# Moving the weight loads of a two-layer decoder step from SyncE's DMA queue to ScalarE's, and four weight tiles later in each chunk

## The reference

```python
# layer 0: differential attention, sample rows read a paged K/V cache of 2048 tokens per sequence
proj = rms_norm(x, norm_pre) @ w_in              # 2048 x 8192: q, k, v, gate
p = softmax(q1 k1^T - slope*dist) - lam * softmax(q2 k2^T - slope*dist)
x = x + rms_norm((head_rms_norm(p @ v) * silu(gate)) @ w_out, norm_post)
# layer 1: retention in chunks of 128, sample rows read and write a recurrent state
proj = rms_norm(x, norm_pre) @ w_in_ret          # 2048 x 12288: q, k, v (512 a head), gate
o = (q k^T * decay) v + q S * decay ;  S = decay*S + k^T v
x = x + rms_norm((head_rms_norm(o) * silu(gate)) @ w_out_ret, norm_post)
```

## Time and profile before

| | us |
| --- | --- |
| median of 3 runs | 4121.02 |
| lowest and highest | 4120.16, 4127.6 |
| the profiled execution's own time | 4107.18 |
| its span | 4105.4 |
| TensorE busy | 3767.5 (92%) |
| ScalarE busy | 1138.2 (28%) |
| VectorE busy | 1427.7 (35%) |

### The profile page before, as it was taken

How to read it: one execution, slowest core, us unless ns; L and a number is a source line. 1 busy time by engine, 2 the same in 40 slices (tenths; PEclk the granted TensorE clock), 3 DMA queues, 4 the chain that set the end, 5 groups by cost and what they waited for, 6 DMA issues and landing times.

```text
span 4105.4 us, 69674 instructions
## 1 busy us (share of the span) xinstructions
PE 3767.5 (92%) x26880; PEld 3289.5 (80%) x26880; DVE 1427.7 (35%) x2278; ACT 1138.2 (28%) x1905; POOL 125.1 (3%) x76
## 2 busy tenths in 40 slices
PE   2998999999999998999579999999999999989996
PEld 2987777777777776776579989898988888879996
DVE  2234333333343334333432423233333334233333
ACT  4233223322332333231332222222222222222221
POOL 0000000200020002002000000000000000000000
PEclk7999999999999998999789999999999999999998
DMA  2355777677767775764323334343424243343323
GB/s 75 106 173 164 233 214 236 190 232 221 238 191 235 218 231 182 228 191 147 113 73 112 125 117 134 111 145 95 154 80 157 79 153 104 133 140 116 106 83 129
DMA packets 466203, 632.41 MB, mean 154 GB/s; under 512 B 39441, under 2 KB 288914, under 8 KB 462738
## 3 DMA queue, kind: packets, MB, share of 16 engines
q1 hardware_dynamic: 401538, 555.71, 43.4%
q10 hardware_dynamic: 64336, 72.24, 5.1%
HBM read 555.61 MB, written 70.65 MB: 153 GB/s over the span
## 4 chain that ended last, share of the span: by engine, by line
PE 53%; DVE 3%; ACT 2%; issue 2%; ACTq 2%; DMA 1%; POOL 1%; SPq 1%; DVEq 0%; POOLq 0%
PE low_banks L832 42%; PE high_banks L832 7%; PE high_banks L835 3%; POOL area L1644 1%; DVE area L1583 1%; ACTq L1245 1%; DVE WL L1328 1%; ACT XH L1055 1%; DVE area L1605 1%; DMA area<-in_cache_v 0%; ACTq L1215 0%; ACT WH L1055 0%; ACTq L1214 0%; PE low_banks L835 0%; ACT area L1055 0%
## 5 line engine op out<-in xcount | busy, mean ns | idle before, releaser
L832 PE MATMUL low_banks<-XH,WH 128*128 128x288 f32 x6656 | 1527.0, 311 | 46.2 <-DVE XL L1333 16.3
L832 PE MATMUL low_banks<-XH,WL 128*128 128x288 f32 x6656 | 1431.9, 297 | 0.0
L832 PE MATMUL low_banks<-XL,WH 128*128 128x288 f32 x6656 | 1428.8, 296 | 0.0
L832 PEld LDWEIGHTS low_banks<-XH,WH 128*128 128x128 f32 x6656 | 1072.5, 191 | 197.0 <-issue 154.5
L832 PEld LDWEIGHTS low_banks<-XH,WL 128*128 128x128 f32 x6656 | 1077.4, 190 | 0.0
L832 PEld LDWEIGHTS low_banks<-XL,WH 128*128 128x128 f32 x6656 | 1077.3, 190 | 0.0
L1328 DVE TENSOR_TENSOR WL<-WR,WH 128x1024 fp32r<-128x1024 f32 x416 | 509.3, 1224 | 965.2 <-ACT WH L1055 964.1
L1055 ACT ACTIVATE WH<-WR 128x1024 fp32r<-128x1024 f32 x416 | 439.9, 1057 | 981.4 <-PE low_banks L832 672.7
L832 PE MATMUL high_banks<-area 128*32 128x512 f32 (+7 forms) x3696 | 670.2, 553 | 45.2 <-issue 17.0
L835 PE MATMUL high_banks<-eye_sb,area 128*128 128x128 f32 (+2 forms) x3048 | 458.8, 287 | 203.2 <-ACT area L1055 150.1
L835 PEld LDWEIGHTS high_banks<-eye_sb,area 128*128 128x128 f32 (+2 forms) x3048 | 362.7, 147 | 346.4 <-issue 182.2
(11 more groups left out here) (93 smaller groups left out, 901.1 us busy)
## 6 DMA issues: line engine op xcount, KB each, us to landing
area<-in_cache_k SPq DMA_DIRECT2D x512, 256.0 KB, 4.1
area<-in_cache_v SPq DMA_DIRECT2D x512, 256.0 KB, 3.9
WR<-in_w_in_ret SPq DMA_DIRECT2D x192, 512.0 KB, 3.6
WR<-in_w_in_attn SPq DMA_DIRECT2D x128, 512.0 KB, 5.2
out<-area ACTq DMA_DIRECT2D x73, 512.0 KB, 3.9
area<-in_state_ret SPq DMA_DIRECT2D x64, 512.0 KB, 5.5
WR<-in_w_out_ret SPq DMA_DIRECT2D x64, 512.0 KB, 3.4
WR<-in_w_out_attn SPq DMA_DIRECT2D x32, 512.0 KB, 4.9
```

Source lines behind the costliest of these rows:

```text
L832: return nc.tensor.matmul(out, a, b, start=start, stop=stop, skip_group_check=True)
```

## The change

`load_w` becomes a stage of ScalarE, and stands behind tile 6 of a chunk in place of tile 2. The split stays where it is. What the load waits for, what it moves and where it goes stay the same; the three loads of `begin` keep their places in the list, now on ScalarE.

```diff
@@ Projections.tile
         out = [Stage("project", **a)]
         if i == 2 and n + 1 < len(self.chunks):
-            out += [Stage("split_w", slot=(n + 1) % 2)] + self.load(n + 3)
+            out += [Stage("split_w", slot=(n + 1) % 2)]
+        if i == 6:
+            out += self.load(n + 3)
@@ block.sync
-            def load_w(g, slot, w, row, col):
-                sp.wait_ge(sem["w_lo"], c.before("w_lo"))
-                sp.dma_start(WR[:, slot, :, :], weights[w][:, row:row + CH, col:col + 256]).then_inc(sem[f"w_in{slot}"], 16)
@@ block.scalar
+            def load_w(g, slot, w, row, col):
+                act.wait_ge(sem["w_lo"], c.before("w_lo"))
+                act.dma_start(WR[:, slot, :, :], weights[w][:, row:row + CH, col:col + 256]).then_inc(sem[f"w_in{slot}"], 16)
```

More of the change, by code:

```diff
@@ L814, in x_tile @@
                     load_x(t, None)
-            run(sp, c, dict(relay_area=all_done(sp, c), relay_loads=all_done(sp, c), load_w=load_w, load_x=load_gated, load_k=load_k, load_v=load_v, load_bias_sample=load_bias_sample,
+            run(sp, c, dict(relay_area=all_done(sp, c), relay_loads=all_done(sp, c), load_x=load_gated, load_k=load_k, load_v=load_v, load_bias_sample=load_bias_sample,
                                   load_bias_prompt=load_bias_prompt, load_head=load_head, load_state=load_state,
@@ L1284, in store_x @@
                 act.dma_start(dst, xt[0:R, t % 2, :]).then_inc(sem[f"x_out{t % 2}"], 16)
-            run(act, c, dict(relay_area=all_done(act, c), split_w=split_w, split_x=split_x, split_s=split_s, evacuate=evacuate, p_exp=p_exp, p_transpose=p_transpose,
+            run(act, c, dict(relay_area=all_done(act, c), load_w=load_w, split_w=split_w, split_x=split_x, split_s=split_s, evacuate=evacuate, p_exp=p_exp, p_transpose=p_transpose,
                                 natural=natural, store_natural=store_natural, store_gated=store_gated, page=page,
```

## The result

The changed kernel takes 4131.4 us (median of 20 runs, 4124.5 to 4135.6) against 4119.6 us for the kernel before on the same chip (20 runs). The ratio is 1.0025, with a 95% interval of 1.0018 to 1.0032. So it is slower: by 11.8 us between the medians, by 10.3 us by the ratio, and between 7.4 and 13.2 by its interval. Predicted were 4114 us, range 4104 to 4127.

The account below looks back on a forecast made before the run. TensorE was taken to set the time, with queue changes moving only its stalls. Terms −2.5 − 2.8 − 4.5 + 1.8 + 0.5 + 0.7 gave −6.8 us, so 4114 us from the median 4121.0; range 4104 to 4127.

Parts of the forecast that it names:

- The start, −2.5: First normalization: the fourth x tile, no longer held behind a weight load on SyncE, starts 2.5 us earlier.
- K pages, −2.8: Attention pairs and tail: K pages issued earlier without weight loads on SyncE, taking 2.8 of 11.6 us of TensorE's waits.
- V pages in the tail, −4.5: Attention's tail: five weight issues leave SyncE (2.4 us) and some late landings come back, 4.5 us gained in all.
- Four evacuations, +1.8: End of each pair's first half: the load's issue pushes a ScalarE evacuation TensorE waits for by 0.45 us, four times.
- One in the tail, +0.5: Attention's tail, 1800.27 to 1800.99 us: a load comes into a gapless stretch of ScalarE on the path, costing 0.5 us.
- State stores: Seven retention heads: a load right behind four state stores takes 1 to 1.5 us to issue, costing nothing.
- waits for VectorE in the heads: Retention heads: a load behind a split waits 1.3 us for VectorE and holds ScalarE 1.8 us, hidden, costing nothing.
- lateness: Weight loads issued 0 to 4 us later still land (3.7 us) before their split, at least 7 us on: nothing.
- sign of error: A profile row in which ScalarE waits for a weight load outside the start would show the prediction wrong.
- Last projection, +0.7: Last projection, near 3610 us: the shifted weight load delays the load of gated values TensorE stalls on, by 0.7 us.
- my rivals: Three alternatives: pages gain all they can (4106, chance 0.25), only issue time returns (4118, 0.2), ScalarE held behind stores (0.08).
- rival 3: Retention heads: ScalarE held behind state stores by 6 us issues, +19 us, 4133 us in all; chance 0.08.

Follow-up runs that it names:

- the start alone: Kernel before, with only the third weight load moved behind the last x tile of the first normalization, still on SyncE; ratio 0.9979.
- the place only: Kernel before, with all weight loads still on SyncE but behind tile 6 instead of tile 2; ratio 1.0007.
- layer 0 alone: Kernel before, with only layer 0's weight loads on ScalarE behind tile 6, layer 1's on SyncE at tile 2; ratio 1.0039.
- the tail alone: Kernel before, with only the 16 weight loads of the tail's V page stretch on ScalarE behind tile 6; ratio 1.0010.
- the small stores: Changed kernel with the prompt's key and value stores cut to 16 of 256 columns; ratio 1.0010 (same cut on the kernel before: 0.9992).
- the turn at tile 2: Only layer 0's loads on ScalarE behind tile 6, each waiting for a semaphore SyncE raises at tile 2 of its list; ratio 1.0031.
- half loads: From the third chunk each weight load brings half its rows; ratio 0.9979 on the kernel before, 0.9989 on the changed one.
- the turn at tile 6: Only layer 0's loads on ScalarE behind tile 6, each waiting for a semaphore SyncE raises at tile 6 of its list; ratio 1.0179.
- layer 1 alone: Kernel before, with only layer 1's weight loads on ScalarE behind tile 6, layer 0's on SyncE at tile 2; ratio 1.0003.

## Why the prediction was wrong

**The start, −2.5: right.** Measured 2.6 us. The larger part of the 8.5 us was given away by the change itself, which put the two first loads and the wait for VectorE on ScalarE's path; the start alone, without them, gains it.

**K pages, −2.8: wrong, the step that failed.** I reasoned that without the weight load's wait and issue "all of them come 0.9 + 0.4 = 1.3 us earlier", and that the waits shrink by it. I kept their landing time at the old value. That is what failed, and it can be read at the very wait that I worked the term out from the earlier trace rows. Here are TensorE's stalls there before, with the change, and with the place only:

```profile
347.55 1.76 PE L835 MATMUL high_banks<-eye_sb,area 128*128 128x128 f32 x7 [3.82 <-DMA area<-in_cache_k]
```
```profile
345.44 1.98 PE L833 MATMUL high_banks<-eye_sb,area 128*128 128x128 f32 x8 [4.28 <-DMA area<-in_cache_k]
```
```profile
346.24 0.66 PE L837 MATMUL high_banks<-eye_sb,area 128*128 128x128 f32 x4 [1.81 <-DMA area<-in_cache_k]
347.68 1.12 PE L837 MATMUL high_banks<-eye_sb,area 128*128 128x128 f32 x4 [0.78 <-DMA area<-in_cache_k]
```

The awaited page was issued 1.5 us ahead of the stall's beginning before, 2.1 us ahead with the change and 2.8 us with the place only, and took 5.2, 6.4 and 4.6 us to land. With the load on SyncE behind this page, the 1.3 us do come, and the wait is 1.2 us shorter. With the load on ScalarE (issued at 334.76, the page at 339.02) 0.7 us come, the landing takes back 1.2, and the wait grows. At 593.86 it is the same: 0.7 us earlier, landing 2.1 us longer. The bytes removed from SyncE's queue stood ahead of the same pages on another one, in part together with the store. At full clock the pairs are 7.0 us longer; 1.4 are the evacuations' (three of the four lie in this stretch), so some 5.6 are left for the pages, which were to gain 2.8. (By TensorE's row their waits grew by 7.1.) My own ends for this term were 0 and −6: I had put the possibility that the weight's bytes hit other pages into the V term and not here, where DMA is busiest (share 0.75 in the earlier trace rows).

**Half clock, not in the sum.** The traces give half the clock behind some of the stalls of 1 us and more. Two such stretches of the changed kernel, after the stalls of 3.04 us at 1187.35 and 1.39 at 1416.95, and then the same places of before; the last three columns are clock, DMA share and GB/s (before had half the clock near the first place too, behind a stall of 2.58 us, but only until 1189):

```profile
1188.00:1198.00 10.00, 9.16 (x46) 8.77 (x46) 3.43 (x9) 4.30 (x8) 10.00 (x1) 0.56 0.23 70
1417.00:1425.00 8.00, 6.53 (x35) 5.49 (x36) 1.14 (x3) 0.97 (x2) 0.00 (x0) 0.60 0.81 258
```
```profile
1189.00:1199.00 10.00, 9.64 (x75) 8.86 (x79) 4.58 (x9) 5.09 (x10) 7.03 (x1) 1.00 0.51 161
1411.00:1422.00 11.00, 9.64 (x77) 7.18 (x78) 1.83 (x4) 0.97 (x2) 0.00 (x0) 1.00 0.82 259
```

In the pairs, half the clock was granted for 44.4, 47.8 and 44.4 us in three kernels with the change in layer 0, and for 30.7, 30.7, 41.0 and 47.8 in four without it there. Half the difference of the means, 45.5 less 37.6, is 4 us. The groups overlap, so this term is likely but not shown.

**V pages in the tail, −4.5: no gain.** The stretch took 71.5 us in the changed kernel, 70.5 with layer 0 alone, 71.1 with the tail alone and 70.7 with the small stores, against 70.2 to 70.8 with an unchanged tail. (With the turn at tile 2 it took 69.1; that one isn't explained.) So neither the part for landing nor that for five issues came, and a loss can't be told from the spread. The half loads show that there is something to gain: 70.0 to 66.7 us with half the bytes. The rule of the Trainium skill that I set beside it (the page "DMA: Bandwidth & Descriptors", Issuing engines are not separate DMA queues) was the better guide in speaking against a gain of landing, and the trace agrees in that; that the sequencer's time would be saved showed only with the smaller loads.

**Four evacuations, +1.8: right.** The stall of 2.58 us in the earlier trace rows is 3.05, behind an issue of 0.48 us:

```profile
1598.42 0.48 ACTq L1063 DMA_DIRECT2D WR<-in_w_out_attn  x1
1599.03 0.41 ACT L1114 ACTIVATE area<-low_banks 128x288 f32<-128x288 f32 x1 [1.05 <-issue]
```
```profile
1600.27 1.19 PE L830 MATMUL high_banks<-area 128*128 128x128 f32 x4 [3.05 <-issue]
```

**One in the tail, +0.5: the place right, the size not.** TensorE's wait there grew from 3.05 us to 4.5 to 4.7, in each of the five kernels with this load on ScalarE at tile 6 at full size (the turn at tile 6 apart), and in the one with half loads. ScalarE's timeline shows that it wasn't the issue of 0.37 us but the wait for VectorE's part ahead of the next evacuation (for the same evacuation see the earlier trace rows):

```profile
1812.74 0.37 ACTq L1063 DMA_DIRECT2D WR<-in_w_out_attn  x1
1813.52 0.41 ACT L1114 ACTIVATE area<-low_banks 128x288 f32<-128x288 f32 x1 [1.72 <-DVE XL L1335]
```

**State stores, waits for VectorE in the heads, lateness: right at nothing, the last by luck.** Behind four stores the load's issue takes 1.25 us, within my 1 to 1.5; why it takes longer there than elsewhere (0.38) no run shows:

```profile
2537.84 3.13 ACTq L1247 DMA_DIRECT2D out<-area  x4
2541.01 1.25 ACTq L1063 DMA_DIRECT2D WR<-in_w_in_ret  x1
```

The row that I had named as a sign of error did appear, ScalarE waiting for weights in the heads of retention:

```profile
ACT WH L1053 <- DMA WR<-in_w_in_ret: 55.4, 9, 7.2
```

I had set lateness at nothing because a load lands in 3.7 us. The median is still 3.6 us in the heads, but the slowest took 10.6 in place of 6.6. It cost TensorE nothing that can be seen: from the split of chunk 200 to that of chunk 351 the trace has 1208.4 us before and 1208.5 after, and layer 1 alone is at 1.0003 (0.9994 to 1.0013). What spared it was the slack behind ScalarE's split and not, as I had reasoned, the slack ahead of it.

**Last projection, +0.7: nothing measured.** ScalarE's wait for the gated values is 4.93 us; it was 4.91.

The sum from the runs: −2.6 (start) + 7.0 (pairs at full clock) + 0.5 (the fourth evacuation, behind them) + 1.7 (tail) + 4 (half clock, likely) = +10.6, beside the 11.8 measured. The 1.7 is one wait; the stretch around it, from the split of chunk 128 to that of 160, took 375.2 us at full clock against 373.1 before, but 374.8 and 374.9 in two executions where it is unchanged. None of my rivals was this case: rival 3 had the sign, with another mechanism. That the weight load could hurt the pages of the pairs had no place in the list.

## What to carry to other kernels

Before a bulk transfer is moved off a queue, ask which transfers it would stand behind there, and which stand between it and the one that is needed next. One queue is also an order: on SyncE a weight load behind tile 6 could not pass the pages that stood ahead of it, on ScalarE's queue it did. In these runs issue time saved on SyncE counted where the order held or the bytes were halved, and was eaten by later landings elsewhere, so a stretch with a DMA share near 0.75 is to be costed with landing times that change. A stage that waits for another engine belongs on an engine whose queue holds nothing urgent; and where a move seems to gain through one freed wait, as at the start here, try that reordering alone first.

## What the runs showed of the hardware

- With a 512 KB load issued 2.2 us ahead on the other queue, and a 256 KB store 0.4 us ahead of that, a K page took 8.0 us from issue to landing in place of 5.8, and the next one 8.8 in place of 6.4.
- Over 440 K pages, one that had a 512 KB load under way at its issue took 5.1 us in the median, one that had none 3.8.
- In the retention heads, where the states come on SyncE's queue and the weights on ScalarE's, the median from issue to landing of a state (512 KB) went from 5.5 to 10.0 us, and no engine's wait for one shows.
- At full clock, four pairs of some 1377 us repeat within 1.5 us over four executions, while the clock moves them by up to 8.6 us (30.7 to 47.8 us at half of it).
